# Banded attention of layer 2 with keys on partitions: transposed scores of four heads, the maximum as contraction rows, sums by GpSimd

## The reference

```
s_ctx = jnp.einsum('bnqhgd,bchd->bnhgqc', qb, kc).astype(jnp.float32) * GQA_SCALE
s_band = jnp.einsum('bnqhgd,bnkhd->bnhgqk', qb, kb).astype(jnp.float32) * GQA_SCALE
valid = (jnp.abs(qpos - kpos) <= WINDOW) & (kpos >= 0) & (kpos < n)
s_band = jnp.where(valid[None, :, None, None], s_band, -jnp.inf)
p = jax.nn.softmax(jnp.concatenate([s_ctx, s_band, s_sink], axis=-1), axis=-1).astype(v.dtype)
o = (jnp.einsum('bnhgqc,bchd->bnqhgd', p[..., :nc], vc)
     + jnp.einsum('bnhgqk,bnkhd->bnqhgd', p[..., nc:nc + 3 * BLOCK], vb))
y_l = (windowed_gqa(q, k, v, ck, cv, sink_hg) * jax.nn.silu(g)) @ w_out
```

## Time and profile before

| what | value |
|---|---|
| median of 3 runs | 2789.06 us (2788.48 to 2791.36) |
| span of the profiled execution | 2787.8 us |
| PE, PEld, DVE, ACT, POOL busy | 2585.8, 2094.8, 1441.4, 1225.3, 235.9 us |
| banded stage, first mask matmul to first matmul of line 927 | 1174.80 to 1492.65 us |
| DMA | 139.55 MB, mean 50 GB/s |

### The profile page before, as it was taken

The page is one execution under the profiler, slowest core; times in us unless marked ns, Lnnn a source line. Parts: engine busy times, 40 slices in busy tenths (PEclk is TensorE's granted clock), DMA queues, the critical chain, the costliest instruction groups (busy, mean ns, idle before and its releaser), DMA issues. The chain is left out here.

```text
span 2787.8 us, 42260 instructions
## 1 busy us (share of the span) xinstructions
PE 2585.8 (93%) x16411; PEld 2094.8 (75%) x16411; DVE 1441.4 (52%) x2384; ACT 1225.3 (44%) x2333; POOL 235.9 (8%) x300
## 2 busy tenths in 40 slices
PE   5999999999999999998889999899998999998787
PEld 3778987877778989877777888787333887797776
DVE  5213266666655513477775723420677546364762
ACT  6112344544444321166664532220666647333662
POOL 1000020010020000001100000000000010004720
PEclk8999999999999999999999999999999999998889
DMA  7430010000112011100002220011000221111012
GB/s 256 173 138 23 18 33 1 1 1 1 62 69 97 25 61 46 61 2 1 2 2 76 106 76 31 12 50 58 19 1 23 76 80 46 38 46 61 1 54 75
DMA packets 71124, 139.55 MB, mean 50 GB/s; under 512 B 2729, under 2 KB 37954, under 8 KB 70802
## 3 DMA queue, kind: packets, MB, share of 16 engines
q1 hardware_dynamic: 53856, 75.89, 8.0%
q0 software_dynamic: 16832, 60.90, 6.0%
q10 hardware_dynamic: 242, 0.07, 0.0%
HBM read 120.08 MB, written 16.78 MB: 49 GB/s over the span
## 5 line engine op out<-in xcount | busy, mean ns | idle before, releaser
L163 ACT ACTIVATE WORK<-PS 128x512 f32<-128x512 f32 (+5 forms) x315 | 156.4, 496 | 634.9 <-PE PS L795 390.4
L795 PE MATMUL PS<-HT_R,W_R 128*128 128x512 f32 (+1 forms) x896 | 332.4, 371 | 0.0
L794 PE MATMUL PS<-WORK_R,W_R 128*128 128x512 f32 (+1 forms) x736 | 270.3, 367 | 0.0
L793 PE MATMUL PS<-WORK_R,W_R 128*128 128x512 f32 (+1 forms) x672 | 248.7, 370 | 13.4 <-DVE W_R L163 7.2
L163 DVE TENSOR_REDUCE SM<-PS 128x1 f32<-128x1280 f32 (+3 forms) x180 | 199.1, 1106 | 93.9 <-PE PS L1107 48.2
L927 PE MATMUL PS<-WORK_R,HT_R 128*128 128x512 f32 x528 | 210.1, 398 | 8.6 <-DVE W_R L163 7.5
L795 PE MATMUL PS<-W_R,WORK_R 128*128 128x256 f32 (+3 forms) x704 | 214.6, 305 | 0.0
L928 PE MATMUL PS<-WORK_R,MIXT_R 128*128 128x512 f32 x544 | 214.0, 393 | 0.0
L858 PE MATMUL PS<-BASE,WORK 128*128 128x128 f32 (+1 forms) x1270 | 187.1, 283 | 26.8 <-DVE WORK L163 18.5
L929 PE MATMUL PS<-W_R,HT_R 128*128 128x512 f32 x528 | 207.4, 393 | 0.0
L794 PE MATMUL PS<-W_R,HT_R 128*128 128x256 f32 (+2 forms) x688 | 206.2, 300 | 0.0
(11 more groups left out here) (297 smaller groups left out, 5650.8 us busy)
## 6 DMA issues: line engine op xcount, KB each, us to landing
MIXT<-in_w_mod POOLq DMA_DIRECT2D x8, 2048.0 KB, 8.5
x_scratch<-WORK POOLq DMA_DIRECT2D x24, 512.0 KB, 2.9
WORK<-x_scratch POOLq DMA_DIRECT2D x24, 512.0 KB, 3.6
W<-in_odd_w_in SPq DMA_DIRECT2D x12, 1024.0 KB, 5.2
W<-in_o_w_in SPq DMA_DIRECT2D x10, 1024.0 KB, 5.3
W<-in_even_w_in SPq DMA_DIRECT2D x5, 2048.0 KB, 7.7
W<-in_w_mod SPq DMA_DIRECT2D x4, 2048.0 KB, 20.6
WORK<-in_x POOLq DMA_DIRECT2D x16, 512.0 KB, 7.9
```

Source lines behind the costliest of these rows:

```text
L163: self.last = Signalled(self, issue(*args, **kwargs))
L793: mm(out, a[0], b_[0], start=k == 0, stop=False)
L794: mm(out, a[1], b_[0], start=False, stop=False)
L795: return mm(out, a[0], b_[1], start=False, stop=k == KT - 1)
```

## The change

The 64 pairs become 16 groups m = (t, gp) of eight heads: four query heads each on two key-value heads, one of these on rows 0 to 63 and one on rows 64 to 127 (`par`). A step n = (m, k) is one key tile of one group; there are 76 steps. The scores are formed transposed, keys on the output's partitions and 4 x 128 queries moving, so that the exponential's output (128 x 1024) feeds the values matmul as it stands and nothing is transposed. The maximum then can't be ACT's bias. It is found beforehand by a second, one-pass product of the high parts with queries on partitions (`gqa_top`, units u = 0 to 3, and u = 4 for the fifth key tile), reduced by DVE, and enters the scores as a fourth pass, a contraction with rows of -max (`FOUR_ROWS_R` by `SHIFT`). Sums over keys: POOL adds the exponentials of a group's steps, a matmul with ones adds over partitions (`gqa_totals`), ACT inverts by exp(-ln). The TOPS place (two banks) has one buffer; z has two (two banks each); output and sum have one bank each. Keys get low parts and are no longer doubled (2 transposes a tile, not 4). Query chunks are loaded by two DMAs each, with 128 columns a piece, and the rotary step of queries runs in two calls of half the heads.

```
 for n in range(NCT, NT + 2):
-    transposes(("gkt", n - 2), [KN2[n % 2][:, k * P:(k + 1) * P] for k in range(GKV)], "act")
+    transposes(("gkt", n - 2), [KN2[n % 2][:, k * P:(k + 1) * P] for k in range(GKV // 2)], "dve")
...
+def gqa_scores(n):
+    m, k = gsteps[n]
...
+    if n >= 2:
+        pe.wait_ge(weighed, n - 1)
+    banded = tile >= NCT and tile - NCT != t
+    if banded:
+        for par in range(2):
+            mm(heads4(z[:, 512 * par:512 * par + 512]), WIN_BF[:, win * P:(win + 1) * P],
+               ID_BF.unsqueeze(1).to_broadcast([P, 4, P]), start=True, stop=False, skip_group_check=True)
+    for step, (a_, b_) in enumerate(((kh, GQH[m % 2]), (kl, GQH[m % 2]), (kh, GQL[m % 2]), (FOUR_ROWS_R, SHIFT[m % 2][:, 0:512]))):
...
+        if k == 0 and step == 3:
+            pe.wait_ge(tops_taken, tops_before["rows", m, 0] + 1)
+        for par in range(2):
+            ins = mm(z[:, 512 * par:512 * par + 512], halves(a_, par), halves(b_, par), start=step == 0 and not banded,
+                     stop=step == 3, skip_group_check=True)
+def open_tops(what):
+    if filled[0]:
+        pe.wait_ge(tops_taken, filled[0])
+    filled[0] += 1
+def gqa_top(m, u):
...
+    for j in range(2):
+        if lo + j != t:
+            for par in range(2):
+                mm(bank(par, CTX + j * P, P), ID_BF, WIN_BF[:, win * P:(win + 1) * P], start=True, stop=False, skip_group_check=True)
+    for par in range(2):
+        mm(bank(par, 0, CTX), q(par, u), keys(par, 0, CTX), start=False, stop=True, skip_group_check=True)
+    for par in range(2):
+        mm(bank(par, CTX, 2 * P), q(par, u), keys(par, CTX + lo * P, 2 * P), start=False, stop=True, skip_group_check=True).then_inc(tops_filled, 1)
+def gqa_rows(m):
+    open_tops(("rows", m, 0))
+    pe.wait_ge(rows_ready, m + 1)
+    nc.tensor.transpose(TOPS[:, 0:P], ROWS[m % 2], IDENT).then_inc(tops_filled, 2)
+def gqa_values(n):
+    pe.wait_ge(weighed, n + 1)
+    if k == 0 and m:
+        pe.wait_ge(out_taken, m)
+    for par in range(2):
+        for i in range(2):
+            last = mm(by_column_half(GOUT, par, i), VG[:, tiles[k], kv * GD:(kv + 1) * GD], head_halves(halves8(GPT[n % 3]), par, i),
+                      start=k == 0 and par == 0, stop=k == len(tiles) - 1, skip_group_check=True)
+XX+for n in range(G_STEPS + 2):
+    if n < G_STEPS:
+        gqa_scores(n)
+    gqa_tops(n, 0)
+    if n >= 2:
+        gqa_values(n - 2)
+    for m in after_group(n, 3):
+        gqa_totals(m)
+    gqa_tops(n, 1)
```

```
+def gqa_weigh(n):
+    act.wait_ge(scored, 2 * (n + 1))
+    if n >= 3:
+        act.wait_ge(valued, n - 2)
+        act.wait_ge(summed, adds_through[n - 3 if gsteps[n - 3][1] else n - 2])
+    f(GPT[n % 3], z_of(n), ACT.Exp, scale=G_SCALE).then_inc(weighed, 1)
+for n in range(len(gsteps) + 2):
...
+    gqa_weigh(n)
+    if k == 0 and m + 1 < len(groups):
+        group_high_parts(m + 1)
+    if k == 3 and m + 1 < len(groups):
+        gqa_sinks(m + 1)
+    if k in (1, 2) and 2 <= m and slabs_done < 2 * KT and (m >= 8 or slabs_done < KT):
+        split_high(f"o_out{slabs_done // KT}", slabs_done % KT)
+    for m in after_group(n, 4):
+        gqa_invert(m)
```

ACT's `gqa_sinks` waits for `tops_ready` and has two small exponentials; `gqa_invert` is Ln and Exp of 128x512. DVE and then POOL:

```
+def gqa_shift(m):
+    if has_tail(t):
+        v.tensor_tensor(TOP, TOP, TAIL, ALU.max)
+    v.scalar_tensor_tensor(rows[:, :, 0:4], heads4(TOP, 2), -1.0, heads4(NEG_SINK[:, 8 * gp:8 * gp + 8], 2), ALU.mult, ALU.min)
+    v.scalar_tensor_tensor(heads4(SINK_T, 2), ..., ALU.mult, ALU.add).then_inc(tops_ready, 1)
+def gqa_rows(m):
+    v.tensor_tensor(heads4(SHIFT[m % 2], 6), TOPS[:, 0:P].unsqueeze(1).to_broadcast([P, 6, P]), heads4(FOUR, 6), ALU.mult).then_inc(tops_taken, 1)
+for n in range(len(gsteps) + 2):
+    for done in after_group(n, 5):
+        gqa_mixed(done)
+    gqa_tops(n, 0)
+    for done in after_group(n, 1):
+        gqa_out(done)
+    if k == 1 and m + 1 < len(groups):
+        group_low_parts(m + 1)
+    gqa_tops(n, 1)
+for n, (m, k) in enumerate(gsteps):
+    if k == 0:
+        continue
+    pool.wait_ge(weighed, n + 1)
+    add_up(total, halves8(GPT[(n - 1) % 3]) if k == 1 else total, halves8(GPT[n % 3]), ALU.add).then_inc(summed, 1)
+    if k == 2 and done < 2 * KT and m >= 4:
+        for _ in range(2):
+            if done < 2 * KT:
+                o_out_low(done)
+                done += 1
```

More of the change, by code:

```diff
@@ L413, in weights @@
             n = chunk_at[name]
-            loads = sum(src is not None for _, src in chunks[n % WS:n + 1:WS])
+            loads = sum(len(src.shape) - 2 for _, src in chunks[n % WS:n + 1:WS] if src is not None)
             eng.wait_ge(w_in[n % WS], 16 * loads)
@@ L618, in has_tail, with keys_of @@
-        def has_tail(p):
-            return n_keys(gqa, pairs[p][0]) > 512
         def near(t):
             return max(t - 1, 0), min(t + 2, NL)
-        def pair_units(p):
-            return 3 if has_tail(p) else 2
-        recip_at = {mla: 0, gqa: 2 * NT}
+        def keys_of(t):
+            return list(range(NCT)) + [NCT + kt for kt in range(*near(t))]
+        def has_tail(t):
+            return len(keys_of(t)) == 5
+        groups = [(t, gp) for t in range(NL) for gp in range(GKV // 2)]
@@ new lines, in build, with group_of_step, after_group @@
+        for n in range(2):
+            tops_in[first_step[-1] + n, 1] = ("gate", n, 0)
+        tops_before, unit_count = {}, 0
+        for m0 in [("top", 0, u) for u in range(top_units(0))] + [("rows", 0, 0)] + [tops_in[key] for key in sorted(tops_in)]:
+            tops_before[m0] = unit_count
+            unit_count += 1
+        all_tops = unit_count
+        def group_of_step(n):
+            return gsteps[n] if n < len(gsteps) else (None, None)
+        def after_group(n, late):
+            return [m for m in range(len(groups) - 1) if first_step[m + 1] + late == n]
@@ L937, in boundary @@
                         behind()
+                    if n == 2 and b == 2:
+                        pe.wait_ge(mixed, len(groups))
                     if n >= 2 and b < 4:
@@ new lines, in _ @@
+            landed(dve, ("gq", NL - 1, 3))
+            for rows in ROWS:
+                v.memset(rows, 0.0)
+            for u in range(top_units(0)):
+                gqa_top(0, u)
+            gqa_shift(0)
+            group_low_parts(0)
+            dve.wait_ge(gqa_const_in, 48)
+            v.tensor_copy(FOUR_ROWS_R, GPT[0][:, 0:P])
+            v.tensor_copy(SINK_SUM_R, GPT[0][:, P:3 * P])
+            gqa_sinks(0)
+            gqa_rows(0)
+            for n in range(len(gsteps) + 2):
+                m, k = group_of_step(n)
+                for done in after_group(n, 5):
[6 more added lines that the diff above has]
+                gqa_tops(n, 1)
+                if (m, k) in ((14, 0), (15, 0)):
+                    gate_diagonal(m - 14)
+                if k == 3 and m in (12, 13):
+                    low_parts(2, NCT + m - 12)
@@ L2655, in _ @@
+            gqa_out(len(groups) - 1)
             dve.wait_ge(layer_done, 2)
-            boundary(2, lambda: gqa_scale(NL - 1))
+            boundary(2, lambda: gqa_mixed(len(groups) - 1))
             for name in r_halves[1:] + ["r_qk", "r_v"]:
```

463 lines of the change are left out of this document (256 added, 207 removed).

## The result

The changed kernel takes 2807.22 us (median of 4 runs, 2803.16 to 2809.59) against 2790.21 for the kernel before on the same chip: a ratio of 1.0059, 95% interval 1.0044 to 1.0074. It is slower by 17 us where 2775 was forecast. The profiled execution has a span of 2807.8 us, 20.0 more than before; it is the slowest of the four (2809.59).

What follows compares the result with a forecast made beforehand. TensorE's order of work was taken to set the banded stage: an inner group of 15.75 us work plus 3.55 waiting, 19.3 against 20.5. From 2789.06, stage -15 and preparation +1 gave 2775 us; range 2735 to 2816, the forecast's own 2760 to 2790.

Steps and rivals of the forecast that it cites:

- A change of shape: TensorE switching between whole array, row halves and column halves, some 28 times a group: about 0.1 us each, within the terms.
- Waits of 3.55: TensorE's waiting in an inner group: 3.55 us beside 15.75 of work, the longest, 1.7, before u2.
- The stage's first groups: First two groups of the banded stage: 14.8 us for the first, 18.2 for the 4-tile group preparing a 5-tile one.
- Rival 1: TensorE's granted clock falls in the stage: at 0.78 about 3 us more a group, +45, 2820; chance 0.15.
- The last group: Last group of the banded stage, which prepares nothing for a next one: 10.5 us.
- Preparation: Work ahead of the stage: key transposes, rotary steps and DMAs, summed with the moved last totals to +1 us.
- The rotary part: DVE's query rotary step in preparation, eight operations for four: +0.65 us a unit, mostly covered, +2.8 in all.
- The other part: Twenty key transposes fewer on TensorE in preparation: -2.4 us, with DVE's low parts of keys taken as covered.
- The moved totals: Last totals, moved: 1.15 us on TensorE in place of eight transposes of about 1.
- Rival 2: Scores matmuls: float32r on row halves runs one after the other, 22 us an inner group, 2816; chance 0.10.
- Rival 3: POOL holds DVE and sums longer in the groups: adds at 2.9, about +0.9 us a group, 2789; chance 0.13.
- Rival 4: TensorE's waits in the groups hide better, so a group nears its 15.75 us of work: 2732; chance 0.18.

Runs made afterwards that it cites:

- e5: Changed kernel with extra float32r matmuls ahead of the first unit of tops, whole-array ones and row-half pairs, alternating and grouped; run once, 2824.1 us, only its timeline used.
- e7: Kernel before with its rotary step of a query unit made in two halves, eight DVE operations for four; 2796.7 us, ratio 1.0014.
- e11: Changed kernel with one rotary call of four DVE operations and four DMAs a query chunk; 2804.9 us, ratio 1.0050.
- e4: Not labelled in the text; by order probably the changed kernel with each tops reduction reading 256 of 1024 columns and the exponent's scale divided by 64; 2778.3 us.
- e13: Changed kernel with the high part of the mix put ahead of the last totals' logarithm and exponential on ACT; 2802.4 us, ratio 1.0039.
- e6: Changed kernel with GpSimd's sums cut to 4 columns in all groups but 0, 1 and 7, exponent's scale divided by 64; 2798.5 us, ratio 1.0030.
- e15: The kernel of e10 with the swap of e13 added; 2765.6 us, ratio 0.9908 to the kernel before.
- e10: Changed kernel with low parts a step earlier, first units in scores buffers, a gate diagonal moved, masks a step ahead, one rotary call; 2769.6 us, ratio 0.9920.

## Why the prediction was wrong

The sign was wrong: 2775 forecast, 2807 measured. For the profiled execution the sum was 2774 and the span is 2807.8; 33.8 us are missing. By its steps:

- **A change of shape at "about 0.1".** This is the step that failed first. It was read from the start of row halves behind two 128-column masks, a difference of two starts in which a mask's own streaming was guessed. Alternating matmuls show 0.184 (e5). Taken for all 24 changes, that is 1.6 of the 1.75 us by which TensorE's work of an inner group was too small; less the 1.15 by which the waits were too large, 0.6 remain (19.9 to 20.1 for 19.3), 7 us over 11 groups, and 10.2 with the slower groups 2 and 4. The prediction put the drain of two records' overlap, 0.16, beside it and went by the other row. The Trainium skill (TensorEngine Tiling (Array Packing), Key Properties) says that changing the tiling mode drains TensorE; e5 agrees in that each change has a cost of its own, 0.184 us. The prediction's sum with a drain of 0.16, 2795, was slower than the kernel before.
- **Waits of 3.55.** Mechanism right: the low parts end 0.55 behind POOL's add, and the longest wait is before unit 2. Its size was 1.10, not 1.7. TensorE's longer work between the fills covers more of each reduction.
- **The stage's first groups, 14.8 and 18.2.** Measured 18.75 and 22.79, 8.5 us more. The first transposes of rows stood 2.4 later than the forecast's mark (1190.96 for 1188.6; where that arose is told under preparation) and group 0 as measured holds one scores step more. The rest is half clock and pauses together: taking the low parts early, which removes a pause of 1.1, made group 1 18.70, where the changed kernel has 22.79 and the three profiles like it 21.2 to 21.6, so shorter by 2.5 to 4.1. How far each feeds the other is not shown. Rival 1 (clock) was thus half right: not in every group, as priced, but for the first 50 us, with a stage clock of 0.94 where 0.92 was given as the point that turns the sign.
- **The last group, 10.5.** Measured 15.37. The sheet left out the two gate rows (1.13 and 1.10) and the values of the last two steps (1.90) that the loop still issues. A plain omission of 4.1 us.
- **Preparation, +1.** The rotary part was right: +2.8 forecast, and the last query transposes moved by 3.0 from e7's edit and by 2.5 from e11's. The other part, -2.4 for twenty key transposes, did not come. From the wait of 3.73 us (see e7) to the last query transposes the kernel before takes 386.7 us, the changed one 390.4 (389.9 to 390.6 in ten more profiles, 387.7 in e4): +3.7, where these two terms gave +0.4. The sheet took DVE's low parts of keys as covered. But each waits for ACT's high part, and the split of the next weight stands behind the last one. DVE and then TensorE in the changed kernel, and TensorE in the kernel before:

```profile
976.29 0.42 DVE L171 TENSOR_TENSOR WORK_R<-PS,WORK_R 128x256 fp32r<-128x256 f32 x1 [2.56 <-ACT WORK_R L171]
976.85 2.56 DVE L171 TENSOR_TENSOR W_R<-W,W_R 128x1024 fp32r<-128x1024 f32 x2
...
978.22 0.55 PE L836 MATMUL PS<-WORK_R,W_R 128*128 128x512 f32 x1 [2.70 <-DVE W_R L171]
```
```profile
979.68 0.47 PE L793 MATMUL PS<-WORK_R,W_R 128*128 128x512 f32 x1 [0.45 <-PE PS L858]
```

  That wait takes 2.2 us, and the 3.4 us behind it run at a granted clock of 0.54, in the kernel before at 1.00 (matmuls 0.43 apart instead of 0.23, about 1.6 us). With e11's single rotary call the distance is still 387.9. No run moved the split, so its price is read from the traces alone.
- **The moved totals.** They were put at the 0.15 by which their matmuls outweigh the ones that they replace; they cost about 5 us (e13). Counted were TensorE's microseconds. Not counted was what is queued behind the waiting instruction on ACT: the high part of the mix, with the low parts and every eviction of the boundary behind it (e13).
- **Rivals 2, 3 and 4.** Rival 2 is refuted (a pair on row halves 0.248). Rival 3: adds were 2.37, not 2.9; the holds exist and cost about 0.5 us a group (e6), and in front of group 15 a held subtraction on 128x8 (1.60 for 0.17) comes with a wait of 1.23. Rival 4 (waits that hide better) did come in part, 2.4 us for 3.55, but on top of more work: it took e15's edits to reach 2766.

Summed: 2.4 at the start, 4.0 and 4.6 in groups 0 and 1, 10.2 in 2 to 12, 2.1 in 13 and 14, 4.9 in 15, 5.9 behind the stage (6.95 less the 1 forecast for all of the preparation and the close): 34.1, against 33.8. The 2.4 at the start are, by the distances above, mostly the preparation's, and of the 5.9 behind the stage about 1 is scatter between profiles. What stays open is how the 8.5 us of groups 0 and 1 divide between the clock and late DVE and POOL in the changed kernel itself.

## What to carry to other kernels

Count changes of the array's shape as instructions with a price of their own, 0.184 us here between the whole array and row halves, before trusting a saving in columns, and order the work so that pieces of one shape lie together. When a step moves, write down on every engine what stands behind the instruction that now waits: two losses that a run took back, 13 and 4 us, were independent work queued behind a late one (reductions behind low parts that POOL's add held, a copy behind the last totals), and each was a one-line swap. The weight split behind a key's low part looks like a third, not tried. The change lost 17 us as it was made and gains 27 by the medians (2792.6 to 2765.6, ratio 0.9908) with the edits of e15.

## What was not expected of the hardware

- A change between the whole array and two row halves costs 0.184 us at full clock, three quarters of a 512-column float32r matmul (0.249); two of these on row halves cost 0.248 together.
- Less work brought more waiting and a lower clock: without the tops' masks the kernel was faster by 7 us by the medians, but the wait before unit 2 grew by 0.56 and the time at half clock from 44 to 65 us.
- One code, two profiles: groups 0 and 1 took 32.9 us at a mean granted clock of 0.93 (e10) and 38.3 at 0.75 (e15), while the four runs of e15 lie within 1 us of one another.
- DVE's four scalings of 128x128 took 3.21 us instead of 1.25 with a POOL add of 2.40 beside them; a subtraction of 128x8 took 1.60 instead of 0.17.
